# The transposed copy in the gated-delta inverse: 32x32 block transposes on VectorE in place of TensorE products

## The reference

```python
a_mat = jnp.where(strict, jnp.einsum('bhnid,bhnjd->bhnij', kbeta, kc) * decay, 0.0)
t_mat = lax.linalg.triangular_solve(a_mat + eye, eye, left_side=True, lower=True)
u = jnp.einsum('bhnij,bhnje->bhnie', t_mat, vc * bc[..., None])
w = jnp.einsum('bhnij,bhnjd->bhnid', t_mat, kbeta * jnp.exp(gcum)[..., None])
```

## Time and profile before

| | |
|---|---|
| median of 3 runs | 1418.44 us (1418.22 to 1422.38) |
| the profiled execution, its own time | 1419.14 us |
| its span in the profile | 1417.3 us |
| PE busy | 1324.0 us, 93% of the span |
| DVE / ACT / POOL busy | 839.8 / 479.8 / 457.5 us |
| chain that ended last | PE 61%, DVE 21%, issue 8%, ACT 6%, POOL 2% |
| mean granted clock of TensorE | 0.971 |

### The profile page before, as it was taken

One profiled execution on the slowest core, in us unless ns is written; L12 is line 12 of the kernel. 1 busy time (PEld: TensorE's weight loads), 2 busy tenths in 40 slices (PEclk: granted clock), 3 DMA queues, 4 the chain that ended last, 5 costly groups with the idle time before them and its releaser, 6 DMA issues.

```text
span 1417.3 us, 28743 instructions
## 1 busy us (share of the span) xinstructions
PE 1324.0 (93%) x10446; PEld 1271.9 (90%) x10446; DVE 839.8 (59%) x1513; ACT 479.8 (34%) x1255; POOL 457.5 (32%) x335
## 2 busy tenths in 40 slices
PE   4999998999899989998999899989998998989997
PEld 4998988898899888988998889889988997989997
DVE  6366377637763786378626862686358635684445
ACT  6242343234323333233323432343243323512210
POOL 0224243423442344234423342334234421432220
PEclk9999999999999999999999999998999898999998
DMA  5332334232423242334233422342233324423253
GB/s 181 117 98 90 94 93 134 85 98 81 146 69 107 84 144 75 104 87 142 77 90 101 135 84 85 107 135 84 71 121 127 99 80 157 141 74 95 91 181 122
DMA packets 84637, 151.81 MB, mean 107 GB/s; under 512 B 10873, under 2 KB 29266, under 8 KB 82962
## 3 DMA queue, kind: packets, MB, share of 16 engines
q1 hardware_dynamic: 74158, 144.87, 32.2%
q10 hardware_dynamic: 10384, 5.50, 1.4%
HBM read 132.19 MB, written 17.27 MB: 105 GB/s over the span
## 4 chain that ended last, share of the span: by engine, by line
PE 61%; DVE 21%; issue 8%; ACT 6%; POOL 2%; DMA 1%; ACTq 0%; DVEq 0%; SPq 0%; POOLq 0%
PE PJ L532 13%; PE PJ L533 13%; PE PJ L534 13%; DVE memx L1405 5%; PE MX L705 3%; PE MX L715 2%; DVE mem L1382 2%; PE MX L720 2%; ACT w_hi L885 1%; PE MX L637 1%; PE MD L757 1%; PE MD L775 1%; DVE memx L1416 1%; DVE memx L1413 1%; ACT mem L1069 1%
## 5 line engine op out<-in xcount | busy, mean ns | idle before, releaser
L532 PE MATMUL PJ<-h_hi,w_hi 128*128 128x260 f32 x2432 | 729.1, 300 | 20.2 <-ACT memx L912 16.8
L533 PE MATMUL PJ<-h_lo,w_hi 128*128 128x260 f32 x2432 | 696.6, 286 | 0.0
L534 PE MATMUL PJ<-h_hi,w_lo 128*128 128x260 f32 x2432 | 695.0, 286 | 0.0
L532 PEld LDWEIGHTS PJ<-h_hi,w_hi 128*128 128x128 f32 x2432 | 468.4, 193 | 41.0 <-ACT memx L912 19.8
L1715 POOL TENSOR_TENSOR w_lo<-w_raw,w_hi 128x512 fp32r<-128x512 f32 (+1 forms) x162 | 218.9, 1352 | 839.6 <-ACT w_hi L885 839.6
L533 PEld LDWEIGHTS PJ<-h_lo,w_hi 128*128 128x128 f32 x2432 | 468.2, 193 | 2.8 <-issue 1.7
L534 PEld LDWEIGHTS PJ<-h_hi,w_lo 128*128 128x128 f32 x2432 | 467.6, 192 | 0.0
L885 ACT ACTIVATE w_hi<-w_raw 128x512 fp32r<-128x512 f32 (+1 forms) x324 | 198.8, 619 | 107.4 <-PE PJ L534 81.1
L1255 DVE TENSOR_TENSOR w_lo<-w_raw,w_hi 128x512 fp32r<-128x512 f32 (+1 forms) x162 | 137.9, 858 | 139.1 <-ACT w_hi L885 133.4
L1405 DVE SCALAR_TENSOR_TENSOR memx<-memx,cw 128x512 f32<-128x512 f32 x72 | 101.1, 1405 | 1.7
L1135 ACT ACTIVATE mem<-MX 128x256 f32<-128x256 f32 x48 | 18.5, 386 | 215.3 <-PE MX L705 215.3
(11 more groups left out here) (306 smaller groups left out, 1761.1 us busy)
## 6 DMA issues: line engine op xcount, KB each, us to landing
w_raw<-in_w_in SPq DMA_DIRECT2D x256, 256.0 KB, 2.6
w_raw<-in_w_out SPq DMA_DIRECT2D x64, 256.0 KB, 2.8
kv<-in_cache_win_k SPq DMA_DIRECT2D x24, 512.0 KB, 3.5
kv<-in_cache_win_v SPq DMA_DIRECT2D x16, 512.0 KB, 3.7
mem<-in_x_prompt SPq DMA_DIRECT2D x4, 1024.0 KB, 11.1
S<-in_state_delta SPq DMA_DIRECT2D x8, 512.0 KB, 3.5
out<-S SPq DMA_DIRECT2D x8, 512.0 KB, 3.7
out<-mem ACTq DMA_DIRECT2D x16, 256.0 KB, 2.3
```

The source lines that it names most:

```text
L532: pe.matmul(out, wh, h_hi[:, k, tok], start=k == 0, stop=False)
L533: pe.matmul(out, wh, h_lo[:, k, tok], start=False, stop=False)
L534: last = pe.matmul(out, wl, h_hi[:, k, tok], start=False, stop=k == KT - 1)
```

## The change

The transposes in slot 39 and ScalarE's copy of them go. In slot 38, VectorE waits for the first `b_U` and makes `b_T` with one instruction that transposes each 32x32 block of the 128x512 fp32 tile in its place. After levels 1 to 4, TensorE's L720 goes (it stays after level 5), and VectorE, once its subtraction of `b_U` has ended, transposes all of `b_U` again instead of subtracting from `b_T`. After level 4 the blocks have size 32, the most that this instruction can transpose.

```diff
@@ TensorE, mix_b
-                pe.wait_ge(s["mix_U0"], h + 1)
-                for c in chunks:
-                    last = pe.transpose(mx(0)[:, c, :], b_U[:, c, :], ident[:])
-                last.then_inc(s["mix_T_ps"], 1)
                 for n in range(1, LEVELS):
...
-                    if n < LEVELS - 1:
+                    if n == LEVELS - 2:
                         for c in chunks:
                             last = pe.matmul(blocks(mx(3)[:, c, :], n, 0), b_U[:, c, :],
                                              blocks(b_Y[:, c, :], n, 0), start=True, stop=True)
@@ ScalarE, mix_b
-                act.wait_ge(s["mix_T_ps"], h + 1)
-                act.activation(b_T, mx(0), ACT.Copy).then_inc(s["mix_T"], 1)
@@ VectorE, mix_b
                 dve.tensor_tensor(sz, xz, ez, ALU.mult).then_inc(s["z_ok_b"], 1)
+                dve.wait_ge(s["mix_U0"], h + 1)
+                dve.transpose(flat(b_T), flat(b_U)).then_inc(s["mix_T"], 1)
                 yield
                 for n in range(1, LEVELS):
                     yield
                     yield
-                    z = (2 * LEVELS - 3) * h + 2 * (n - 1) + 1
-                    dve.wait_ge(s["mix_Z"], z)
-                    if n < LEVELS - 1:
-                        dve.wait_ge(s["mix_Z"], z + 1)
+                    dve.wait_ge(s["mix_Z"], LEVELS * h + n + n // (LEVELS - 2))
                     u = all_blocks(b_U, n, 1)
                     dve.tensor_tensor(u, u, all_blocks(mx(2), n, 1), ALU.subtract).then_inc(s["mix_UT"], 1)
-                    if n < LEVELS - 1:
+                    if n < LEVELS - 2:
+                        dve.wait_ge(s["mix_UT"], UTS * h + 3 * n - 2)
+                        dve.transpose(flat(b_T), flat(b_U)).then_inc(s["mix_UT"], 1)
+                    elif n == LEVELS - 2:
                         t = all_blocks(b_T, n, 0)
                         dve.tensor_tensor(t, t, all_blocks(mx(3), n, 0), ALU.subtract).then_inc(s["mix_UT"], 1)
+                    if n < LEVELS - 1:
                         dve.memset(all_blocks(b_Y, n + 1, 1), 0.0).then_inc(s["mix_UT"], 1)
```

More of the change, by code:

```diff
@@ L283, in blocks, with flat @@
             return x.rearrange("p (k a s) -> p k a s", a=2, s=1 << n)[:, :, odd, :]
+        def flat(x):
+            return x.rearrange("p c d -> p (c d)")
         def all_blocks(x, n, odd):
@@ L306, in build @@
             "hg_ok mix_T1 mix_ss mix_lnrk mix_rs mix_scal mix_gb mix_tok mix_kbT_ps mix_kbT mix_arg mix_D "
-            "mix_kk mix_qk mix_A mix_QK mix_B mix_U0 mix_T_ps mix_T mix_Y_ps mix_Y mix_Z mix_UT ch_kS ch_r "
+            "mix_kk mix_qk mix_A mix_QK mix_B mix_U0 mix_T mix_Y_ps mix_Y mix_Z mix_UT ch_kS ch_r "
             "ch_v_ps ch_v ch_S_ps ch_o_ps ch_S ch_o1 ch_o o_sq on_rs o_n o_T z_sig_b z_ok_b gated_b gB_out S_out "
```

## The result

The changed kernel takes 1443.9 us (median of 4 runs, 1443.6 to 1446.3) where the kernel before takes 1419.9: a ratio of 1.017, 95% interval 1.015 to 1.019. It is 24 us slower; the forecast was 1402.5 us. The profiled execution lasted 1446.3 us, with a span of 1444.5 and a mean granted clock of 0.955 (before 0.971).

A forecast was written before the change was run, and what follows sets the result against it. TensorE, busy 93% of the span, was taken as the bound. From the profiled 1419.1 us, 21.9 saved, 8 added for clock falls and 2 off for re-dealt ones gave 1403.2; less 0.7 to the median, 1402.5 us, range 1392 to 1413.

The forecast's parts named there:

- Slot 38 and 39: Start of the inverse: first transpose moves to VectorE; L705 starts 0.80 us earlier, L775 0.70 in heads that waited for L1773.
- The price of 0.1 us of waiting at L775: Slot 40: TensorE reaches L775 at 549.79 and starts it at 549.90, behind L1560, still before the old 550.59.
- the prediction's own signs of being wrong: Transpose mean above 1 us, L775 starting to wait in slot 40, or TensorE's idle time moving to the tiles' ends.
- rival 1: Slow transpose, about 1.22 us: levels lose, L1560 comes one GpSimd instruction later, L775 too; about 1430 us, chance 0.09.
- The transpose at 0.71 us: VectorE's block transpose, slot 38 and levels 1 to 4: 0.71 us, from the reduction's rate plus a little for filling.
- Rivals 1 and 2: The second: the transpose waits for GpSimd as L1382 does, in slot 38 and level 4; about 1422 us, chance 0.07.
- 0.87 us for each of three levels, 0.40 lost at level 2: Removed L720 groups save 0.87 us at levels 1, 3, 4; level 2, already late on VectorE, costs 0.40 more.
- 0.53 us in slots 38 to 40: Saving per head at the inverse's start: 0.70 us in four heads that waited for L1773, 0.35 in four others.
- falls dealt anew: Existing clock falls redistributed by the shorter head, possibly fewer: 2 us gained, with 5 on either side.
- The clock: Level 2's new 2.1 us gap drops the clock in five heads of eight, up to 1.6 us each: 8 us lost.

## Why the prediction was wrong

The step that failed is the end of "Slot 38 and 39": "L1559 goes at 548.80, and L1560 behind L1791, at 549.80". The first half came true: L1559 took 0.48 us and ended with L1768. The second didn't: L1560 was passed over twice and took 3.2 us instead of 1.0. The price of 0.1 us of waiting at L775 became 2.35 us a head, 18.8 in all, with 6.8 us of half clock around it. A wait of L775 in slot 40 stands among the prediction's own signs of being wrong, without a price or a chance. The same step had the mechanism in rival 1, as something that only a slow transpose would bring; the transpose was fast, and the place that L1560 had come through before was lost all the same. I took it that an instruction with two SBUF inputs waits for the one GpSimd instruction that is running. The earlier trace rows show that for one case and say nothing on the next.

- *The transpose at 0.71 us*: 0.711 and 0.712 measured. Rivals 1 and 2 were wrong; it doesn't wait for GpSimd.
- *0.87 us for each of three levels, 0.40 lost at level 2*: right. No wait stands at levels 1, 3 and 4, and level 2 waits 2.1 us in each head. With the first copy and level 2 on TensorE, 20.2 us came off the inverse against 20.9.
- *0.53 us in slots 38 to 40*: 0.8 us in the heads that had waited for L1773 (20.3 to 19.5 us from T1 to Y1), as forecast, and 2.3 in the other loop heads (21.8 to 19.5), more than the 0.35, because the fall of the clock at L757 was gone there. For falls dealt anew the prediction had 2 us, with 5 on either side, and said nothing on their place; that all four went here is luck.
- *The clock*: the size of a fall was right (1.66 us against 1.6), the count wasn't. Where five falls in eight heads were taken, level 2's gap brought one in each of the eight, and L774's gap brought 6.8 us of half clock more (3.4 in head 0). In the changed kernel the stretch from Y1 to C is 287.7 - 17.7 + 18.8 = 288.8 without the clock, and 323.8 with it: 35.0 us, 4.4 in each head, for 10.2 us at half clock (6.8 in head 0). So the 36.1 us that the inverse lost are 35.0 of clock and 18.8 of the outer product's wait, less 17.7 saved. By the 13.3 us of the kernel with the first copy on TensorE, some 13 of the 35.0 are level 2's and some 22 stand around the outer product, an estimate.
- *Re-dealt falls and other waits*: they are larger than the 2 us with 5 on either side. They took 16.8 us from one version and 9.3 from another, always outside the stretch that was changed. The prediction gave a fall the same price wherever it comes; but in front of T1 it costs nothing, since PE waits there for VectorE in any case, and behind T1 it costs its full price. What decides between the two places stays open, and so does the spread of the kernel with the transpose behind L1560.

## What to carry to other kernels

Work that goes to an engine with time to spare still moves what is queued behind it; ask of each of these instructions what it needs besides its own engine, and whether it comes at the same point of the other engine's run as before. Price a wait of the bounding engine with the clock that falls behind it: here a wait of 2.1 us cost 1.7 us more at half clock, and one of 2.35 us some 2.7. A fall in front of a wait for another engine costs nothing; when it moves behind that wait, it does. A gain in one stretch isn't in hand until the stretches that weren't changed have been timed too; when they take it back, cut the loop at fixed places and compare.

## What the runs showed of the hardware

L1560, a VectorE instruction with two SBUF inputs, went in at the end of a GpSimd instruction of 128 partitions when it had come 0.2 us into it (L1768, L1715: 1.0 and 1.1 us). Having come 0.2 us into one of 8 partitions with another right behind, it was held through that and the two behind it, 3.2 us, in all eight heads; with a pause behind the 8-partition one it took 0.87 us. A block transpose of 128x512 fp32 on VectorE took 0.71 us, in slot 38 beside a GpSimd instruction (0.712) and at the levels (0.711). PE's waits of 2.1 to 2.35 us between dense matmuls came with 3.4 us or 6.8 us at a granted clock of 0.5 in every head of the changed kernel. Over all versions that have it, level 2's wait of 2.1 to 2.2 us brought half clock in 39 of 40 heads, and its wait of 0.8 to 0.9 us in none of 32. But the length of the wait alone doesn't decide: the 2.3 us behind ScalarE's L912 brought half clock before T1 in 52 of 84 heads, and the 1.1 us at the outer product (GpSimd's small product later) in all eight heads that had it.
